# The scores of the dilated attention, two heads in turn on the two halves of the array's rows

## The reference

```
outs = [_dilated_branch(qh, kh, vh, w, d) for (w, d) in ((128, 1), (512, 4), (2048, 16))]
m_all = maximum of the branches' m
num = sum(exp(m - m_all) * acc);  den = sum(exp(m - m_all) * l);  o = num / den
attn = _rms_norm(o, attn_out_gain)
rw = _rwkv7(r, k, v, ...)
mixed = concatenate([attn, rw]) @ w_out
```

## Time and profile before

| | us |
|---|---|
| median of 3 runs | 1532.68 |
| lowest, highest | 1531.84, 1535.1 |
| the profiled execution | 1532.59 |
| its span | 1530.8 |
| PE busy | 1437.6 (94%) |
| DVE busy | 736.2 (48%) |
| ACT busy | 613.0 (40%) |
| POOL busy | 473.7 (31%) |
| mean granted clock of PE | 0.948 |

### The profile page before, as it was taken

How to read it: one execution, slowest core, us unless ns; L and a number is a source line. 1 busy time by engine, 2 the same in 40 slices (tenths; PEclk the granted TensorE clock), 3 DMA queues, 4 the chain that set the end, 5 groups by cost and what they waited for, 6 DMA issues and landing times.

```text
span 1530.8 us, 19427 instructions
## 1 busy us (share of the span) xinstructions
PE 1437.6 (94%) x7762; PEld 1146.2 (75%) x7762; DVE 736.2 (48%) x1176; ACT 613.0 (40%) x960; POOL 473.7 (31%) x172
## 2 busy tenths in 40 slices
PE   6999999899889999999997999999999989699997
PEld 5878877688667888888886888777887867577763
DVE  3355367733354541514215199336353245566664
ACT  4443345322352432323214234654434444365552
POOL 2452023000124664645532454422233520200001
PEclk9999999657898999999998999999999999799998
DMA  6232123000134444444443234211223602889964
GB/s 215 90 117 70 32 88 110 2 1 1 42 138 132 157 136 153 140 149 143 146 150 111 83 108 126 83 55 35 105 83 137 214 11 103 341 333 422 412 270 180
DMA packets 98815, 207.61 MB, mean 136 GB/s; under 512 B 6785, under 2 KB 56321, under 8 KB 92065
## 3 DMA queue, kind: packets, MB, share of 16 engines
q1 hardware_dynamic: 91808, 181.13, 34.5%
q10 hardware_dynamic: 4608, 16.78, 2.8%
q0 software_dynamic: 2304, 8.39, 1.5%
HBM read 170.63 MB, written 35.65 MB: 135 GB/s over the span
## 4 chain that ended last, share of the span: by engine, by line
PE 82%; DVE 6%; ACT 5%; issue 3%; DMA 3%; POOL 1%; SPq 0%; POOLq 0%; DVEq 0%; ACTq 0%
PE bank L517 22%; PE bank L499 13%; PE bank L501 13%; PE bank L500 12%; PE bank L2876 4%; PE bank L809 3%; PE bank L785 3%; PE bank L800 2%; PE bank L1206 2%; ACT whi L428 1%; PE bank L706 1%; PE bank L2813 1%; PE bank L1160 1%; PE bank L1265 1%; PE bank L1280 1%
## 5 line engine op out<-in xcount | busy, mean ns | idle before, releaser
L436 POOL TENSOR_TENSOR wlo<-raw,whi 128x2048 fp32r<-128x2048 f32 (+2 forms) x83 | 378.7, 4562 | 652.7 <-ACT whi L428 616.4
L428 ACT ACTIVATE whi<-raw 128x2048 fp32r<-128x2048 f32 (+1 forms) x84 | 159.1, 1894 | 274.7 <-PE bank L501 267.4
L517 PE MATMUL bank<-alo,whi 128*128 128x512 f32 x368 | 149.2, 406 | 5.0 <-DVE alo L728 5.0
L2005 DVE TENSOR_TENSOR ffn_relu<-ffn_relu 128x512 f32<-128x512 f32 x32 | 97.6, 3051 | 106.7 <-ACT ffn_relu L1985 106.7
L517 PE MATMUL bank<-ahi,whi 128*128 128x512 f32 x368 | 146.5, 398 | 0.0
L499 PE MATMUL bank<-alo,whi 128*128 128x512 f32 (+1 forms) x360 | 141.5, 393 | 0.0
L501 PE MATMUL bank<-ahi,wlo 128*128 128x512 f32 (+1 forms) x360 | 140.3, 390 | 0.0
L500 PE MATMUL bank<-ahi,whi 128*128 128x512 f32 (+1 forms) x360 | 140.1, 389 | 0.0
L517 PE MATMUL bank<-ahi,wlo 128*128 128x512 f32 x368 | 91.7, 391 | 0.0
L517 PEld LDWEIGHTS bank<-alo,whi 128*128 128x128 f32 x368 | 71.3, 194 | 23.5 <-DVE alo L728 6.2
L517 PEld LDWEIGHTS bank<-ahi,whi 128*128 128x128 f32 x368 | 71.2, 193 | 15.5 <-issue 0.7
(11 more groups left out here) (517 smaller groups left out, 2994.0 us busy)
## 6 DMA issues: line engine op xcount, KB each, us to landing
raw<-in_w_in_dram SPq DMA_DIRECT2D x18, 1024.0 KB, 5.3
expert_gate_up<-in_expert_w_gate_dram SPq DMA_DIRECT2D x17, 1024.0 KB, 11.2
expert_gate_up<-in_expert_w_up_dram SPq DMA_DIRECT2D x17, 1024.0 KB, 13.9
expert_down<-in_expert_w_down_dram SPq DMA_DIRECT2D x17, 1024.0 KB, 8.7
raw<-in_w_ffn_up_dram SPq DMA_DIRECT2D x16, 1024.0 KB, 6.2
raw<-in_w_ffn_down_dram SPq DMA_DIRECT2D x16, 1024.0 KB, 5.6
raw<-in_w_in_first_dram SPq DMA_DIRECT2D x12, 1024.0 KB, 5.3
expert_rows_dram<-zero_rows SPq DMA_DIRECT2D x23, 512.0 KB, 6.9
```

The lines of the kernel that those rows point to most:

```text
L428: nc.scalar.activation(whi[:, n % SPLIT, 0:k * c], raw[:, n % RAW, 0:k * c], ACT.Copy).then_inc(hi_made, 1)
L436: nc.gpsimd.tensor_tensor(wlo[:, n % SPLIT, 0:k * c], raw[:, n % RAW, 0:k * c], whi[:, n % SPLIT, 0:k * c].bitcast(F32), ALU.subtract).the ...
L517: ins = nc.tensor.matmul(acc, of, by, start=first and i == 0, stop=last and i == products - 1)
L2005: nc.vector.tensor_tensor(relu2[:, n % 2, :], relu[:, n % 2, :], relu[:, n % 2, :], ALU.mult).then_inc(up_sq, 1)
```

## The change

One argument: the dilated attention's units are planned with `together=2`.

```
-            yield from attn_units("dil", NHEAD, lambda t: (t + 1) * P, lag=2)
+            yield from attn_units("dil", NHEAD, lambda t: (t + 1) * P, lag=2, together=2)
```

## The result

| | before | after |
|---|---|---|
| median of 6 runs, us | 1534.63 | 1542.90 |
| lowest, highest | 1531.84, 1537.32 | 1540.35, 1546.65 |
| profiled execution, span | 1532.59, 1530.8 | 1545.06, 1543.3 |
| mean granted clock of PE | 0.948 | 0.936 |

What follows compares the result with a forecast made beforehand. It took PE to bound the stretch, except DVE from 270 to about 289 us. Terms of +1.5 before the inversion, -0.3 in it and -7.5 behind it gave -6.3, so 1526.3 us; 8-in-10 range 1520.5 to 1533.

Steps and rivals of the forecast that it cites:

- the term for the mask stages, +1.9: Mask stages before the inversion: new waits in steps 5 and 7 and less overlap of scores cost 1.9 us.
- the sum of +1.5 up to the inversion: From 240 us to the inversion's start: start -0.4 and mask stages +1.9, together 1.5 us later; bounds 0 and +3.
- rival 1: Mask stages: the clock falls there, not at 280; if at 264, +3.5 us in all, 1536.1 us; chance 0.10.
- if L1215 runs at the lower clock: L1215, ahead of the inversion: a sign that the prediction is wrong; the forecast had granted clock 1.00 until about 280.
- Start, -0.4: First scores to the first mask product L1198: two pairs are shorter, PE gets there sooner, 0.4 us saved.
- Inversion, -0.3: DVE's chain, 272.7 to 289.1 us: the attention steps inside have 7 tiles instead of 8, saving 0.3 us.
- L1226, +1.4: Behind the inversion: step 14's product with V waits for DVE's read of score 13, so L1226 starts 1.4 us later.
- The third part, -7.5: 289.1 to 384.1 us: scores -11.6, L1226 +1.4, more tiles +0.9, bank waits +3.1, end -1.3; sum -7.5 us.
- rivals 2 and 3: Score pairs: strict order with three passes, 1530.8 us, chance 0.07; or no overlap at all, 1535.3 us, chance 0.03.
- The bank waits, forecast 3.1: Third part: PE waits for DVE at pairs 18/19 and 22/23 and V products 25 and 29: 0.9, 0.8, 0.3, 1.1 us.
- rival 4: Bank waits twice as long, as DVE and ScalarE drift behind PE: +3.5 to +5 us, 1530.5 us; chance 0.12.
- Rival 5: Third part: the clock comes back sooner since pairs fill more of the array; 6 us go, 1520 us; chance 0.06.

Runs made afterwards that it cites:

- the two kernels with pairs and turning: Changed kernel with banks dealt out anew, plus identity transposes where PE stood still: in an extra bank, 1506.18 us; in the next transposes' bank, 1498.64 us.
- the kernel with pairs and turning in a bank of its own: Changed kernel with banks dealt out anew, plus identity transposes into an extra bank behind steps 11 to 14, in the inversion: 1506.18 us, ratio 0.9818.

## Why the prediction was wrong

- **The step that failed** is the term for the mask stages, +1.9, and with it the sum of +1.5 up to the inversion: it took these stages at full clock. They ran at half clock from 253, and the start of the inversion came 19.4 us late. What kept the fall out of the sum is the argument in rival 1, "At 270 to 280 it kept the full clock at 8.0 busy of 10, which speaks against." That stretch has no mask products in it, and what the clock did there did not carry over to holes in the mask stages; why is not shown. The two holes themselves were forecast in place and nearly in size (for step 5, 1.75 us from the transposes to the next mask product, and 1.81 measured, 251.04 to 252.85). What was missing is what they trigger.
- **Rival 1** was the right mechanism, with a chance of 0.10 and the wrong place. It put the fall at 264, counted 9.8 us of work and came to 1536.1; the fall is at the first hole, and L1206 to L1559 went from 24.75 us to 44.67. The sign that the prediction named, "if L1215 runs at the lower clock", is what came true: 7.04 us for 3.74.
- **Start, -0.4:** -0.6 at the first mask product.
- **Mask stages without the holes:** with the banks re-dealt, first L1206 to L1559 takes 24.36 us, 24.75 before: -0.4, where the sum has +0.6 beside the 1.3 for the two waits.
- **Inversion, -0.3:** -0.26 (16.37 to 16.11).
- **L1226, +1.4:** +1.5. It starts 1.55 us behind the end of L1581 (0.05 before), after a wait for the read of score 13.
- **The third part, -7.5:** -7.1 to L1316. The scores take 10.0 us, as forecast. The pair at the price of one product holds (2.01 us on four tiles at the lower clock, where three passes would be 2.8), so rivals 2 and 3 are out. The bank waits, forecast 3.1, are 2.4 (rival 4 is out): 0.46, 0.84 (before 336.20, shown above), 0.15 and 0.94. They came 0.7 us short and the sum still 0.4 over, so other terms came 1.1 us long together, and that the sum is this near is in part luck. The lines of the waits:

```profile
322.96 1.22 PE L785 MATMUL bank<-kt,qt 64*128 64x256 f32 x4 [0.46 <-DVE zr L827]
359.61 1.51 PE L809 MATMUL bank<-vt,zk 128*128 128x64 f32 x6 [0.15 <-DVE zr L827]
381.79 0.41 PE L809 MATMUL bank<-vt,zk 128*128 128x64 f32 x2 [0.94 <-DVE zr L827]
```

- **Rival 5** (the clock comes back sooner): not in the profiled run, in which it returns 3 us behind the first product of L1287, as before; one other execution had 7 us of it, and the two kernels with pairs and turning had most of it.
- What would have changed the forecast: to ask of each new wait not only how long it is, but what the work behind it costs if the clock falls there. Two such waits were in the sum, at +1.3 together; the stretch in which they stand cost 18 us more than the sum had for it.

Not settled: why, by the times, a hole of 0.88 us at 252 leads to a fall in one run of six in one kernel, and one of 0.97 in all 15 of another. The changed kernel has the second wait and other banks beside it; what else differs was not seen. The Trainium skill (TensorE: Matmul & The Clock Gate, Part 1, on what is actually happening) says of the rise to the full clock at a kernel's start that its moment varies from run to run of one kernel. In the changed kernel the dip at 243 varies too: it is in three of four profiles, and the fall stands 0.2, 0.5, 0.5 and 1.5 us behind the end of the hole in them.

## What to carry to other kernels

A wait of under 1 us on TensorE can cost twenty, if the granted clock falls behind it: price every new wait also by what would run at half clock until the clock returns, and read in the windows whether it fell. Interleaving two heads on the two row halves is worth its full saving (a pair for the price of one), but it takes two banks at once, so deal the pair's banks last in the step and check who waits for a score just made. Where TensorE must wait for another engine, harmless products in a bank that is next anyway bought 21 us more in the kernel with pairs; in the one without, fewer of them bought 3.5.

## What the runs showed of the hardware

- The granted clock fell 0.2 to 2.0 us behind the end of a hole of 0.88 to 0.97 us in six profiles. It held over holes of 0.54 and 0.67 in one kernel and of 0.53 and 0.91 in another. In the idle stretches of 4.23 and 2.20 us it fell while PE stood still.
- A busy PE alone does not bring it back: PE was busy 62.00 of 62 us at 0.50 (298 to 360, single heads), and for 37 us of mask and L1215 work with 0.64 us idle (changed kernel). In the twelve profiles in which the clock was at half when L1287's products (K=128, 128 columns) began, it came back 2.1 to 5.0 us behind the first of them. In the kernel with pairs and turning in a bank of its own it came back some 7 and 17 us behind its first two falls.
- It can fall with PE busy 3.69 of the 4 us ahead.
- The dip at 243, which some executions of a kernel have and some don't, lasted 3.4 us in most profiles, about 7 in one and about 10 in another; between two profiles of the changed kernel it made 2.9 us at L1215.
